# The scan's old state moves from TensorE to VectorE, a weight split moves behind the scan's last copy, and GpSimd's bonus product waits for the scan's end

## The reference

```python
def step(S, inp):
    r_t, w_t, k_t, v_t, aa_t, bb_t = inp
    sa = jnp.einsum('bhvk,bhk->bhv', S, aa_t)
    S = S * w_t[:, :, None, :] + sa[..., None] * bb_t[:, :, None, :] + v_t[..., None] * k_t[:, :, None, :]
    y_t = jnp.einsum('bhvk,bhk->bhv', S, r_t)
    return S, y_t
```

## Time and profile before

| | |
|---|---|
| time, median of 3 runs | 1123.92 us (1123.31 to 1125.4) |
| time of the profiled execution | 1125.01 us |
| its span, first to last instruction | 1123.0 us |
| TensorE matmul busy | 1095.9 us (98%) |
| VectorE busy | 687.6 us (61%) |
| ScalarE busy | 503.7 us (45%) |
| GpSimd busy | 92.8 us (8%) |
| mean granted TensorE clock | 0.999 |

### The profile page before, as it was taken

The page is one execution under the profiler, slowest core; times in us unless marked ns, Lnnn a source line. Parts: engine busy times, 40 slices in busy tenths (PEclk is TensorE's granted clock), DMA queues, the critical chain, the costliest instruction groups (busy, mean ns, idle before and its releaser), DMA issues.

```text
span 1123.0 us, 17984 instructions
## 1 busy us (share of the span) xinstructions
PE 1095.9 (98%) x6760; PEld 864.9 (77%) x6760; DVE 687.6 (61%) x1163; ACT 503.7 (45%) x865; POOL 92.8 (8%) x145
## 2 busy tenths in 40 slices
PE   7999999989999999999999999999999999999997
PEld 6887888767777777777766888888888888888886
DVE  4224566678878777787785444547776777752224
ACT  6426555633524445253533333455556555641122
POOL 8100001101010110101110100100000000000000
PEclk9999999999999999999999999999999999999999
DMA  8632333210111111111312544333332333232221
GB/s 212 131 94 76 94 95 94 76 39 20 39 39 48 39 57 57 48 58 39 113 57 86 153 137 131 123 103 103 93 95 83 105 93 97 86 105 94 94 75 75
DMA packets 154390, 97.01 MB, mean 86 GB/s; under 512 B 30761, under 2 KB 143575, under 8 KB 154327
## 3 DMA queue, kind: packets, MB, share of 16 engines
q1 hardware_dynamic: 148800, 79.72, 24.5%
q0 software_dynamic: 5376, 16.37, 4.6%
q10 hardware_dynamic: 151, 0.04, 0.0%
HBM read 87.71 MB, written 8.39 MB: 86 GB/s over the span
## 4 chain that ended last, share of the span: by engine, by line
PE 88%; DVE 7%; ACT 1%; DMA 1%; issue 1%; SPq 1%; DVEq 0%; ACTq 0%
PE ps L1607 15%; PE ps L1610 15%; PE ps L1609 15%; PE ps L1590 5%; PE ps L2086 4%; PE ps L2087 4%; PE ps L2085 4%; PE ps L1592 4%; PE ps L1591 4%; PE ps L1734 3%; PE ps L1884 2%; PE ps L1863 1%; PE ps L1688 1%; PE ps L1819 1%; PE ps L1682 1%; DMA raw<-in_w_in 1%
## 5 line engine op out<-in xcount | busy, mean ns | idle before, releaser
L1096 DVE TENSOR_TENSOR wlo<-raw,whi 128x1024 fp32r<-128x1024 f32 x142 | 173.5, 1222 | 214.2 <-ACT whi L691 141.7
L691 ACT ACTIVATE whi<-raw 128x1024 fp32r<-128x1024 f32 x124 | 131.1, 1057 | 133.1 <-PE ps L1610 124.5
L1607 PE MATMUL ps<-xnh,whi 128*128 128x512 f32 x344 | 136.0, 395 | 0.0
L1610 PE MATMUL ps<-xnh,wlo 128*128 128x512 f32 x344 | 135.9, 395 | 0.0
L1609 PE MATMUL ps<-xnl,whi 128*128 128x512 f32 x344 | 135.9, 395 | 0.0
L1607 PE MATMUL ps<-xh,whi 128*128 128x512 f32 x248 | 99.7, 402 | 3.0 <-DVE xl L1114 1.7
L1610 PE MATMUL ps<-xh,wlo 128*128 128x512 f32 x248 | 97.9, 395 | 0.0
L1609 PE MATMUL ps<-xl,whi 128*128 128x512 f32 x248 | 97.8, 394 | 0.0
L1590 PE MATMUL ps<-xh,whi 128*128 128x512 f32 x184 | 88.6, 481 | 0.0
L1610 PEld LDWEIGHTS ps<-xnh,wlo 128*128 128x128 f32 x344 | 64.6, 188 | 15.8
L1607 PEld LDWEIGHTS ps<-xnh,whi 128*128 128x128 f32 x344 | 64.6, 188 | 15.6
(11 more groups left out here) (335 smaller groups left out, 2211.8 us busy)
## 6 DMA issues: line engine op xcount, KB each, us to landing
raw<-in_w_in SPq DMA_DIRECT2D x108, 256.0 KB, 3.2
raw<-in_w_up SPq DMA_DIRECT2D x88, 256.0 KB, 3.1
raw<-in_w_down SPq DMA_DIRECT2D x44, 256.0 KB, 2.8
gates_scratch<-gst POOLq DMA_DIRECT2D x16, 256.0 KB, 2.4
raw<-in_w_proj_b SPq DMA_DIRECT2D x16, 256.0 KB, 4.0
raw<-in_w_proj_a SPq DMA_DIRECT2D x16, 256.0 KB, 3.0
gl<-gates_scratch POOLq DMA_DIRECT2D x16, 256.0 KB, 3.1
raw<-in_w_out SPq DMA_DIRECT2D x16, 256.0 KB, 3.0
```

Source lines behind the costliest of these rows:

```text
L691: act.activation(flat(whi[:, hb]), flat(raw[:, b]), ACT.Copy).then_inc(w_hi, 1)
L1096: dve.tensor_tensor(flat(lo[:, hb]), flat(raw[:, b]), flat(hi[:, hb]).bitcast(F32), ALU.subtract).then_inc(w_lo, 1)
L1607: pe.matmul(ps[bank][:, :], whi[:, hb, k, :], hi(k), start=first and k == 0, stop=False)
L1610: ins = pe.matmul(ps[bank][:, :], wlo[:, hb, k, :], hi(k), start=False, stop=last and k == kn - 1)
```

## The change

- In chunks 1 and 2 TensorE no longer adds the old state with the identity. VectorE multiplies the old state by the decay into a new tile `decayed` (128x128, while the sum is still being made), waits for itself, and writes the new state as decay x sum + `decayed` on the two 64x64 diagonal blocks, one instruction for each. In chunk 0 it is two multiplications on the two blocks. The blocks off the diagonal are cleared once, by GpSimd's memset of `stm` in place of one of `zp`.
- The split of weight tile `N_FILL + 3n` leaves the third place of VectorE's list and comes after the u copy of chunk 3; the place after the z copy of chunk 3 is left empty. The seven pieces behind it each move one place forward.
- GpSimd's bonus product waits, from the second pair on, for the u copy of chunk 3.

```diff
@@ gpsimd
             def bonus_product(n):
                 pool.wait_ge(kmod_ready, n + 1)
+                if n:
+                    pool.wait_ge(u_ready, n * NT)
                 pool.tensor_tensor(z[:, n + 8, :], z[:, n, :], kmod[:, :], ALU.mult)\
                     .then_inc(rk_product, 1)
...
-            pool.memset(zp[:, :], 0.0).then_inc(cleared, 1)
+            pool.memset(stm[:, :, :], 0.0).then_inc(cleared, 1)
@@ vector, scan
                     if j < NT - 1:
+                        gain = carry[:, d % 2, j + 1:j + 2]
+                        if j:
+                            dve.wait_ge(s_ready, d * (NT - 1) + j)
+                            dve.tensor_scalar(decayed[:, :], stm[:, j % 2, :], gain, None, ALU.mult)\
+                                .then_inc(s_decayed, 1)
+                            dve.wait_ge(s_decayed, d * (NT - 2) + j)
                         dve.wait_ge(s_ps, d * (NT - 1) + j + 1)
-                        dve.scalar_tensor_tensor(stm[:, (j + 1) % 2, :], ps[4 + j % 2][:, 0:P],
-                                                 carry[:, d % 2, j + 1:j + 2], headones[:, :],
-                                                 ALU.mult, ALU.mult).then_inc(s_ready, 1)
+                        for h in range(2):
+                            hs = slice(h * HD, (h + 1) * HD)
+                            dst, src = stm[hs, (j + 1) % 2, hs], ps[4 + j % 2][hs, hs]
+                            if j:
+                                ins = dve.scalar_tensor_tensor(dst, src, gain[hs], decayed[hs, hs],
+                                                               ALU.mult, ALU.add)
+                            else:
+                                ins = dve.tensor_scalar(dst, src, gain[hs], None, ALU.mult)
+                        ins.then_inc(s_ready, 1)
                         fill()
@@ vector, main
-                scan(n - 1, prep[:2] + [lambda: weights(N_FILL + 3 * n)] + prep[2:])
+                scan(n - 1, prep + [lambda: None, lambda: weights(N_FILL + 3 * n)])
@@ tensor, scan
                     if j < NT - 1:
-                        if j:
-                            pe.matmul(zb, ident[:, :], stm[:, j % 2, :], start=True, stop=False)
-                        pe.matmul(zb, ktok[:, j, :], vp[:, j, :], start=j == 0, stop=False)
+                        pe.matmul(zb, ktok[:, j, :], vp[:, j, :], start=True, stop=False)
```

More of the change, by code:

```diff
@@ L221, in build @@
         stm = take("stm", [P, 2, P])
+        decayed = take("decayed", [P, P])
         rkones = take("rkones", [P, P])
@@ L349, in build @@
         s_ready = sem("s_ready")
+        s_decayed = sem("s_decayed")
         out_ps = sem("out_ps")
```

## The result

The change made the kernel slower: 1132.59 us median against 1124.35 for before (nine runs each), a ratio of 1.0083 with a 95% interval of 1.0057 to 1.0110. The prediction was 1122.7 and a range up to 1125.2. What stands out is the spread: the runs before lie within 1122.75 to 1125.84, those after run from 1126.28 to 1138.27, and each lies on a level of TensorE's mean granted clock. One run had 1.000 (1126.28), five 0.991 or 0.992 (1130.8 to 1134.3), three 0.985 or 0.986 (1137.4 to 1138.3). So two things have to be found: some 2 us that are there without any loss of clock, and 6 or 12 that come with it.

The account below looks back on a forecast made before the run. TensorE, busy 98% of the span, gains only where it stands still, chiefly waiting for z copies. Middle scans -1.8, first +0.05, last +0.53 sum to -1.2 us: 1122.7 from 1123.92, 8-in-10 range 1120.5 to 1125.2.

Parts of the forecast that it names:

- +0.53 for the last scan: Last scan: `decayed` and the second half come on top, +0.40 in chunk 1 and +0.13 in chunk 2.
- The new state copy: VectorE, chunks 1 and 2: `decayed` 0.23 and halves 0.28 each, state ready at U + 1.65 and U + 1.54.
- The late load: Line 1877, chunk 1: weights no longer loaded early cost 0.06 a middle scan; the matmul's turn not missed, chunk 2 free.
- Middle scans: Scans d = 1 to 6: each gains 0.36 - 0.06 = 0.30, six gain 1.8 us.
- the gain of the moves: Middle scan: 0.11 at chunk 1's z copy from the split, 0.25 at chunk 2's from the bonus product.
- First scan: Without filler to hide the later state, gains and losses at the z copies and loads sum to +0.05.
- the identity's product: TensorE, chunks 1 and 2: removal worth 0, hidden behind the u copy, bounds 0 and 4.3 us; rival chance 0.20.
- the product's collision with `removed`: Chunk 2's z copy: `removed` took 1.66 instead of 0.68 beside GpSimd's product; 0.25 a scan lost there.
- the split and the product behind the scan: After chunk 3's u copy: cost 0, split keeps 1.22 and GpSimd waits; collision rival up to +1.4, chance 0.05.
- signs of being wrong: Profile after: TensorE idle before line 1877, earlier u copy, split over 2 us, or last scan longer by over 0.6.
- low edge of 1121.5: Lower end of the forecast's own range: no late load and cheap halves (-2.2), and 0.2 less in the last scan.
- The first rival: Line 1877, chunks 1 and 2: dearer state copy makes TensorE wait; upper bounds +6.1, middle 1125.7, chance 0.20.

Follow-up runs that it names:

- mere lateness: Kernel before, with unused VectorE multiplications ahead of each state copy in the last scan alone, making the state late: 1125.07 us, ratio 1.0014.
- the moves alone: Kernel before with only the weights split behind the last u copy and the bonus product at the scan's end: 1121.31 us, ratio 0.9978.
- the multiplication ahead of the u copy: Change with the old state copy in the last scan; in the others `decayed` is computed before the u copy, not behind the following piece: 1121.60 us, ratio 0.9979.
- part 7: Whole change with the last scan's y_lo pieces moved to where VectorE stands idle: 1125.41 us, ratio 1.0024.

## Why the prediction was wrong

**The step that failed first is one that it does not have.** The sum priced each late copy at its own length: +0.53 for the last scan. That TensorE's idle time there could halve its clock for the following filler work, and cost 6 us more, stands neither in the sum nor among the rivals; the loss of clock was put at nothing without a reason. Restoring the last scan took most of the loss away (1123.14), the new last scan alone brought it into before (1131.15), with useless products in both scans the longest of ten runs took 1127.02, and mere lateness brought falls, though smaller and rarer ones. The profile before had the place in it: of all eight scans the first and the last have the least filler, and TensorE already waited for the state there, 0.60 in the last scan (599.71, above) and behind the state copy of the earlier trace rows in the first.

**The new state copy was mis-sized.** The start U of its chunk, the u copy's, is where the working put it, and so is `decayed` (U + 0.93 against U + 0.91). I had 0.23 for `decayed`; it took 0.28. I had the halves 0.20 apart with the next piece 0.20 behind the second; they took 0.58 together, 0.29 apart, and the next piece started 0.61 behind the first (I had 0.40). The state was ready at U + 1.83 in chunk 1 and U + 1.70 in chunk 2 (predicted 1.65 and 1.54). The steps of a long VectorE queue, where an independent instruction begins 0.08 before the other's end, did not hold for 64-column halves. The late load that the working charged with 0.06 a scan cost 0.35: 0.17 + 0.04 for a missed turn, which it had excluded, and 0.07 in each of two chunks for weights that were not loaded early, which it had in one.

**What each scan made of it.** Middle scans: the gain of the moves, 0.36, is as predicted in sum (its parts were not: 0.05 in chunk 1 in place of 0.11), and the state copy took 0.33 to 0.35 of it in place of 0.06; their six together took 286.65 where they had taken 286.57, so 0.0 a scan in place of -0.30. First scan: +0.39 in place of +0.05. Last scan, with the clock up: from its first z copy to the filler behind its outputs 14.76 in place of 13.20, +1.56 in place of +0.53. By the z copies chunk 0 lost 0.46, which the working left at nothing: its two halves pushed a 1.22 piece, and that the z copy. Chunk 1 lost 0.80 in place of 0.40 and chunk 2 0.30 in place of 0.13. Together +2.0 without any fall, which agrees with the two runs of the change at a clock of 0.999 and more, 1126.3 and 1124.4, and with 1125.6 where TensorE is kept busy.

**Right:** the identity's product is worth 0; the product's collision with `removed` cost the z copy what it was said to, and the moves together win; the split and the product behind the scan cost nothing, with the product blocked behind the split (1.22 and 2.11); the moves alone give -2.3 us. Two of its signs of being wrong came true: TensorE idle before line 1877 by more than 0.1 in the middle scans (0.17 in chunk 1), and a last scan longer by more than 0.6.

**A slip in the range.** Its low edge of 1121.5 takes 2.2 and 0.2 off the time before and leaves out the sum's own +0.05 and +0.53. With them it is 1122.1. Nothing else hangs on it, as the miss is at the other end.

**The first rival,** a dearer state copy, had the right place and the right sign for the 2 us, with a chance of 0.20. Its price, 1125.7, lies between the two runs of the change without a fall. That is partly luck: it was meant for up to 16 places of all eight scans, and 1.6 of the 2.0 us came from the last scan alone.

**Open.** That the lowest level, 0.986, is a fall in both scans fits two losses of 0.007, but no profile of such a run was taken. Why the same idle time brings a fall in one run and none in another, and what sets its length, wasn't tried. With both scans kept busy the falls are gone in ten runs, against 13 of 15 runs of the change (clock of 0.994 or less), so that idle time is what brings them is shown; which of the waits counts most is not. With the moves alone and with the multiplication ahead of the u copy no fall was seen in 19 runs, which bounds its rate but doesn't exclude it.

## What to carry to other kernels

A wait of the matmul engine costs its own length only as long as its clock holds: where a stretch has little filler, about a microsecond more of idle time, spread over several waits, can halve the clock for the work behind it, and then even useless products are worth their price. Here they brought most of the loss back, but not all of it: 1125.6 against 1123.4 for before. A spread of the runs in steps, each with its own mean clock, is the sign to look for. And when work moves from a busy engine to an idle one, it is its place in that engine's queue that counts: the new state copy cost 0.35 a middle scan with its multiplication behind a piece, and 0.10 with it in front of the wait for the u copy, ahead of that piece.

## What the runs showed of the hardware

TensorE's granted clock fell from 1.00 to 0.50 behind waits of 0.60, 0.40 and 1.16 us that followed each other closely, and stayed there for 17 us in one profile, for 7 in another, although TensorE was at work for 16.83 of the 17.30 us from 600.7 to 618. In the first scan a single named wait of 0.75 (with the reordered last scan, part 7) came ahead of a fall of about 14 us. From a scan's first matmul to the last wait ahead of a fall TensorE had been busy for 0.6 to 1.3 us less than before: 6.29 in place of 6.97 in the first scan, 5.89 in place of 7.16 in the last, 6.53 with mere lateness. A pair of 128-column products took 0.77 in place of 0.46, a filler matmul of 512 columns 0.63 in place of 0.40. The same timing of the instructions came with a fall in one profile and without in another, in both scans (waits of 1.16 and of 0.75 in the same places).

Two VectorE instructions on 64x64 blocks at different partitions did not overlap, neither with each other (0.58 for two of 0.283) nor with the next; on 128 columns and more the next started 0.08 before the end.

The order in which VectorE and GpSimd came to a pair of two-input instructions decided which one waited: product first, `removed` took 1.66; split first, the product took 2.11 and the split 1.22. The Trainium skill (SBUF — State Buffer, Who interferes with whom) states this rule, and these runs agree in both orders.
